# Adding two branches' shares to a tile by accumulating transfers from GpSimd

## The reference, cut to what matters

```python
gates = jax.nn.sigmoid(merge.reshape(B, S, N_BRANCH, D))     # N_BRANCH = 4, D = 2048
y = jnp.einsum('bsnw,nwd->bsnd', branches, w_branch[l])      # 512 -> 2048 for each branch
mixed = jnp.sum(gates * y, axis=2) @ w_mix_out[l]
x = layer_norm(DEEPNORM_ALPHA * x + mixed, ln_mix_g[l], ln_mix_b[l])
```

## Time and profile before

| | us |
|---|---|
| three timed runs, median | 3278.08 |
| lowest and highest | 3277.97, 3278.86 |
| span of the profiled execution, first to last instruction | 3274.4 |
| TensorE busy in it | 3231.5 |
| VectorE busy | 2023.5 |
| ScalarE busy | 1353.6 |

### The profile page before, as it was taken

The page is one execution under the profiler, slowest core; times in us unless marked ns, Lnnn a source line. Parts: engine busy times, 40 slices in busy tenths (PEclk is TensorE's granted clock), DMA queues, the critical chain, the costliest instruction groups (busy, mean ns, idle before and its releaser), DMA issues.

```text
span 3274.4 us, 41325 instructions
## 1 busy us (share of the span) xinstructions
PE 3231.5 (99%) x17441; PEld 2781.1 (85%) x17441; DVE 2023.5 (62%) x1659; ACT 1353.6 (41%) x908; POOL 0.2 (0%) x4
## 2 busy tenths in 40 slices
PE   9999999999999999999999999999999999999998
PEld 8888888887888888888888888788888988888886
DVE  7566566667686666665465786674556544445556
ACT  4333555433344444443333443343333444444332
POOL 0000000000000000000000000000000000000000
PEclk9999999999999999999999999999999999999999
DMA  8645456677556555555645545564454655555553
GB/s 314 216 154 183 173 210 214 213 270 274 198 188 205 186 182 195 177 201 194 219 173 192 173 172 192 201 219 167 155 189 171 219 185 187 192 185 187 194 194 138
DMA packets 284856, 642.80 MB, mean 196 GB/s; under 512 B 11032, under 2 KB 16964, under 8 KB 273732
## 3 DMA queue, kind: packets, MB, share of 16 engines
q1 hardware_dynamic: 270000, 587.50, 52.4%
q10 hardware_dynamic: 14740, 53.59, 4.4%
HBM read 622.18 MB, written 18.87 MB: 196 GB/s over the span
## 4 chain that ended last, share of the span: by engine, by line
PE 91%; DVE 5%; ACT 1%; issue 1%; DMA 1%; ACTq 0%; DVEq 0%
PE ps L1149 46%; PE ps L1049 40%; PE ps L1044 4%; ACT whi L628 1%; PE ps L1153 1%; DVE wlo L1656 1%; DVE m_t L1720 0%; DMA wraw<-in_xattn_v 0%; DVE tok L1892 0%; DVE tok L1897 0%; DVE act_hl L1720 0%; DVE tok L1720 0%; DVE tok L2572 0%; DMA d_bias<-bias_dram 0%; DVE tok L2571 0%
## 5 line engine op out<-in xcount | busy, mean ns | idle before, releaser
L1656 DVE TENSOR_TENSOR wlo<-wraw,whi 128x2048 fp32r<-128x2048 f32 x549 | 1244.8, 2279 | 707.2 <-ACT whi L628 699.8
L628 ACT ACTIVATE whi<-wraw 128x2048 fp32r<-128x2048 f32 x549 | 1042.3, 1906 | 1381.0 <-PE ps L1149 624.7
L1149 PE MATMUL ps<-act_hl,whi 128*128 128x512 f32 (+1 forms) x3872 | 904.7, 380 | 0.6 <-DVE m_k L1767 0.6
L1149 PEld LDWEIGHTS ps<-act_hl,whi 128*128 128x128 f32 x3872 | 698.5, 188 | 125.8 <-DVE m_k L1767 0.7
L1049 PE MATMUL ps<-whi,act_hl 128*128 128x512 f32 x2128 | 661.8, 392 | 0.9 <-DVE wlo L1656 0.6
L1149 PE MATMUL ps<-act_hl,wlo 128*128 128x256 f32 x3664 | 499.1, 283 | 0.0
L1149 PEld LDWEIGHTS ps<-act_hl,wlo 128*128 128x128 f32 x3664 | 481.3, 191 | 17.3
L1049 PEld LDWEIGHTS ps<-whi,act_hl 128*128 128x128 f32 x2128 | 396.1, 188 | 83.7 <-issue 1.9
L1049 PE MATMUL ps<-wlo,act_hl 128*128 128x512 f32 x1064 | 414.4, 390 | 0.0
L1049 PE MATMUL ps<-whi,f_h 128*128 128x512 f32 x672 | 261.4, 389 | 0.0
L1049 PE MATMUL ps<-whi,f_l 128*128 128x512 f32 x672 | 261.4, 389 | 0.0
(11 more groups left out here) (324 smaller groups left out, 2062.2 us busy)
## 6 DMA issues: line engine op xcount, KB each, us to landing
wraw<-in_w SPq DMA_DIRECT2D x132, 1024.0 KB, 5.1
wraw<-in_w_in SPq DMA_DIRECT2D x118, 1024.0 KB, 5.3
wraw<-in_ffn_in SPq DMA_DIRECT2D x88, 1024.0 KB, 5.0
wraw<-laid_narrow_units SPq DMA_DIRECT2D x68, 1024.0 KB, 4.8
wraw<-in_ffn_out SPq DMA_DIRECT2D x44, 1024.0 KB, 5.0
wraw<-in_w_branch SPq DMA_DIRECT2D x16, 1024.0 KB, 5.1
wraw<-in_w_mix_out SPq DMA_DIRECT2D x16, 1024.0 KB, 5.1
wraw<-in_w_out SPq DMA_DIRECT2D x16, 1024.0 KB, 5.1
```

The lines of the kernel that those rows point to most:

```text
L628: act.activation(whi[:, slot, k, c], wraw[:, slot, k, c], ACT.Copy).then_inc(hi_done, 1)
L1149: return pe.matmul(o, left, right, start=start, stop=stop, skip_group_check=True)
L1656: dve.tensor_tensor(wlo[:, slot, k, c], wraw[:, slot, k, c], whi[:, slot, k, c].bitcast(F32), ALU.subtract).then_inc(lo_done, 1)
```

## The change

The second and third branch (n = 1, 2): VectorE still writes its product into m_t, but m_t now has four buffers, one for each column block (16 KB instead of 4 KB in each partition), and VectorE adds nothing. It signals share_ready; GpSimd waits for this and issues a transfer from m_t[:, cb] to tok[:, cb] with accumulate-add, which signals share_added[cb] when it has landed. Before the second accumulation into a column GpSimd waits for the first one; before VectorE writes m_t[:, cb] again, for n = 2 and 3, it waits for the earlier accumulations of that column. The fourth branch is added by VectorE as before.

```diff
-        m_t = place("m_t", Y1 + 8 * KB, [P, 1, NT, UNIT])
+        m_t = place("m_t", Y1 + 8 * KB, [P, NB, NT, UNIT])
...
+        share_ready = sem("share_ready")
+        share_added = [sem(f"share_added{q}") for q in range(NB)]
...
+        @block.gpsimd
+        def _(pool):
+
+            for n in range(1, 3):
+                for cb in range(NB):
+                    pool.wait_ge(share_ready, NB * (n - 1) + cb + 1)
+                    if n > 1:
+                        pool.wait_ge(share_added[cb], 16)
+                    pool.dma_start(tok[:, cb], m_t[:, cb], accum_op=ALU.add).then_inc(share_added[cb], 16)
...
-                    kept(tt((m_t if n else tok)[:, 0 if n else cb], x, two(m_g[:, k % 2, :]), ALU.mult))
+                    if n > 1:
+                        dve.wait_ge(share_added[cb], 16 * (n - 1))
+                    kept(tt((m_t if n else tok)[:, cb], x, two(m_g[:, k % 2, :]), ALU.mult))
                     dve.sem_inc(gate_used, 1)
-                    if n:
-                        x = tt(tok[:, cb], tok[:, cb], m_t[:, 0], ALU.add)
-                        if n < 3:
-                            link(x)
-                        else:
-                            x.then_inc(normed, NT)
-                            dve.wait_ge(normed, NT * (NB + cb + 1))
+                    if n == 3:
+                        tt(tok[:, cb], tok[:, cb], m_t[:, cb], ALU.add).then_inc(normed, NT)
+                        dve.wait_ge(normed, NT * (NB + cb + 1))
+                    elif n:
+                        dve.sem_inc(share_ready, 1)
```

## The result

The changed kernel takes 3286.61 us (median of 15 runs, 3284.31 to 3289.93), the kernel before on the same chip 3278.72 us (15 runs, 3275.61 to 3283.96). The ratio is 1.0025, 95% interval 1.0019 to 1.0032: it is slower by 0.25%, some 8 us. I had said 3277.5 us, no change, and had given 0.14 to a time above 3284.6.

What follows compares the result with a forecast made beforehand. TensorE, busy 3231.5 of 3274.4 us, bounds the kernel; in the merge a ring of VectorE and ScalarE paces it. 3278.08 less 0.57 for the adds, all else 0 or hidden, gave 3277.5 us, range 3277.0 to 3278.4.

Steps and rivals of the forecast that it cites:

- The removed adds: VectorE, branches two and three: eight adds hidden while ScalarE rounds weights; removal wins 0.071 us a column, 0.57 us.
- The added waits and GpSimd's issue at nothing: Merge: VectorE's waits for accumulations, some 22 us after asking, and GpSimd's issuing of transfers were both taken to cost 0.
- The rival of GpSimd's descriptor work in VectorE's way: After the product: GpSimd's issue work delays VectorE beyond its freed 2.5 us; at 4 us, 3289 us; chance 0.04.
- I take one copy per accumulation: DMA engines in the merge: each accumulation costs 1.34 us of all engines, all traffic hidden; chance 0.50.
- the rival's price: Two copies, 2.7 us per accumulation: weight load behind x_again 3.8 to 6.5 us late, 3278 to 3284 us; chance 0.32.
- the room of 3.0 MB before 728.70: DMA engines, 704.80 to 728.70: 265 of 391 GB/s used, room for four accumulations of 2.1 MB at one copy each.
- No more than 2.9 us can be won in the stage at all: TensorE in the merge: its idle time, 0.68 + 2.20 = 2.9 us, was taken as the bound on any gain.
- the sign of being wrong: Merge: whi released by a transfer, product waiting for a gate or accumulation, or wlo above 2.29 us would refute the forecast.
- passes 7.1 us from 2.1 copies on: Weight load behind x_again, three-or-more-copies rival: lateness 8 x 1.34c less 7.7 and 7.3 us; 3288 to 3295 us; chance 0.11.

Runs made afterwards that it cites:

- no_adds: Kernel before with the eight adds of branches two and three left out, nothing in their place: merge stretch 0.57 us shorter, ratio 0.9999.
- tiny: Changed kernel with each accumulation cut to 2 x 16 of a partition's 1024 elements: merge stretch 0.57 us shorter than before, ratio 1.0000.
- plain_copy: Changed kernel with a plain copy of the same bytes in place of each accumulation: merge stretch 1.10 us longer than before, ratio 1.0002.
- only_second: Changed kernel with accumulating transfers for the second branch alone, VectorE adding the third: merge stretch 0.25 us shorter than before, ratio 0.9999.
- hi_first: Kernel before with ScalarE rounding the next weights before it waits to issue the gate load: 3273.51 us against 3278.34, ratio 0.9988.
- half_acc: Changed kernel with each accumulation for the first 128 tokens only, half the bytes: merge stretch 0.70 us longer than before, ratio 0.9999.
- only_third: Changed kernel with accumulating transfers for the third branch alone, VectorE adding the second: merge stretch 7.22 us longer than before, ratio 1.0021.
- after_x_early: Changed kernel with x_again's four loads issued one by one in the first branch's columns: merge stretch 2.03 us longer than before, ratio 1.0002.

## Why the prediction was wrong

- **The removed adds: right.** Eight adds, 9.8 us, in the shadow of whi; 5.893 us a column; 0.57 us won, shown by no_adds and tiny.
- **The added waits and GpSimd's issue at nothing: right.** tiny has them all and loses nothing. The rival of GpSimd's descriptor work in VectorE's way is out by the same run; wlo still takes 2.29 us. The Trainium skill's inference (SBUF — State Buffer, "Who interferes with whom") that descriptor writing doesn't take the port of wlo's second input is not tested by it: GpSimd's work ends before wlo begins (707.66 and 708.66 in the changed kernel, 708.44 and 709.10 in tiny), so the two never met.
- **"I take one copy per accumulation": this is the step that failed.** I took 1.34 us of all engines and hid all of it. It measured 2.64 us against 1.30 for a copy, two copies, which was the rival's price, and it was not hidden: the first w_mix_out load came 8.5 us late. The Trainium skill (Collectives: The Full Stack, section on the bandwidth ceiling and the fold count) says that a reducing transfer reads two sources and so delivers half the rate of a copy; the traces agree, 2.64 us to 1.30.
- **The rival's own size was too small.** At two copies I had the load land in 23.2 to 25.9 us and the kernel at 3278 to 3284 us; it took 25.2 and 3286.6. But I had it issued at 734.93; x_again's blocked issue made that 737.12, so from the place where I had it issued it took 27.4 us, and whi was 8.5 us late, not 3.8 to 6.5. And I left out what the idle time does to TensorE's clock: at half clock for 2 us and at 0.76 on average for 7 more, the transposes and the next column take 0.9 + 1.75 us longer. The sum, by places: whi is 8.5 us behind its rhythm, 7.9 behind the kernel before (less the 0.57 won); TensorE still had work for 0.46 of it, so its second transposes come 7.4 us later than before; at the third it is 9.3, by the clock's part, of which a wait of 0.62 us for VectorE goes off that the kernel before has there and this one hasn't (and 0.2 us of overlap). That is the measured + 9.32.
- **Even at one copy the sum was not right.** plain_copy is that case: I had 16.1 us and no stall, it was 19.7 us and + 1.10 us. The step that failed there is the room of 3.0 MB before 728.70, from which I took four copies (2.1 MB) for nothing. The bytes do fit: until x_again comes, SP's loads don't fall further and further behind. But they take 10.1 to 11.4 us to landing from the first copy on, instead of 5.0 to 5.2, and with this delay of some 5.7 us the queue enters the stretch of x_again. Bytes that are free on average do not say how long a load takes. With accumulations there isn't even the room: by the measured costs SP's queue is left 5.9 - 1.3 - 2.6 = 2.0 us of each column, for 1.05 MB of weights, which took it 2.8 us (by 39.8% of 27 us for 3.97 MB), so it falls behind: in the changed kernel the loads issued from 711 to 729 take 10.8, 11.7, 14.3 and 16.1 us. The rise is not in every run (14.7, 16.1, 14.2 and 11.0 in only_second), so this last count is an estimate and not shown in full.
- **"No more than 2.9 us can be won in the stage at all"** was wrong too: hi_first won 4.54. In this forecast it bounded only the chances of a gain.
- **Where the loss lies** (first w_mix_out load, whi released by a transfer, wlo before the product) was the place that I named as the sign of being wrong, so the place was right. The point ("passes 7.1 us from 2.1 copies on") was not: by the same count the measured 2.64 us each make 8 x 2.64 - 15.0 = 6.1 us late, and it was 8.5.

What stays open: that GpSimd's and ScalarE's queues keep their pace (8.6 and 7.5 us) while SP's loses is shown by shares and landings; why the engines divide their time so was not tried. The Trainium skill (DMA: Bandwidth & Descriptors, "Queues, rings and completion order") tells of turns between the queues, a packet of several descriptors each; the shares of 45.0 and 39.8% neither show nor exclude such turns, since no run varied the size of the packets alone.

## What to carry to other kernels

Before you take work off an engine, look whether the engine waits right behind it: here 9.8 us of adds were worth 0.57, and moving one wait in ScalarE's order was worth 4.5. Price an accumulating transfer as two copies (measured for 512 KB within the core's memory), and ask what the slowest queue has left per step while it runs, not how many bytes are free on average. Then look for the one load that stands behind something that can wait: with the accumulations there, x_again's place made 7 of the 9 us, and without them none.

## What the runs showed that I had not expected

- SP's issue of a transfer can block: x_again's fourth took 5.99 us in the changed kernel, four issues 7.68 instead of 2.33, and w_mix_out's next issues 2.2 to 7.7 us, while its queue was behind.
- Time to landing says little of a queue's cost: 16 KB accumulations landed in 7.3 us (tiny), 256 KB in 8.5 (half_acc) and 512 KB in 8.6, at no cost, + 0.7 and + 9.3 us.
- The chain from a late load has a tail in the clock: 7.86 us idle, then granted clock 0.50 in 769.20 to 771.20; only_third shows the same behind 5.72 us idle, after_x_early, with waits of up to 2.0 us, doesn't.
